# Three gate chunks per layer as seven block products in a streaming encoder on one Trainium2 core

## What is computed

```python
gates = jax.nn.sigmoid(g.reshape(bsz, t_len, N_BRANCH, D_MODEL) + b_gate)
merged = (gates[:, :, 0] * (y_a @ w_branch[0])
          + gates[:, :, 1] * (y_b @ w_branch[1])
          + gates[:, :, 2] * (y_c @ w_branch[2]))
x = layer_norm(DN_ALPHA * x + merged @ w_out, ln1_g, ln1_b)
```

## Time and profile before

| what | value |
|---|---|
| median of 3 runs | 1741.15 us (1741.02 to 1742.72) |
| the profiled execution's own time | 1741.31 us |
| its span | 1739.6 us |
| PE busy | 1725.9 us, 99% of the span, 13778 matmuls |
| DVE busy | 1365.6 us, 78% |
| ACT busy | 856.9 us, 49% |
| POOL busy | 101.6 us, 6% |
| DMA | 186.00 MB, mean 107 GB/s |

### The profile page before, as it was taken

How to read it: one execution, slowest core, us unless ns; L and a number is a source line. 1 busy time by engine, 2 the same in 40 slices (tenths; PEclk the granted TensorE clock), 3 DMA queues, 4 the chain that set the end, 5 groups by cost and what they waited for, 6 DMA issues and landing times.

```text
span 1739.6 us, 32719 instructions
## 1 busy us (share of the span) xinstructions
PE 1725.9 (99%) x13778; PEld 1692.2 (97%) x13778; DVE 1365.6 (78%) x1967; ACT 856.9 (49%) x1402; POOL 101.6 (6%) x159
## 2 busy tenths in 40 slices
PE   9999999999999999999999999999999999999997
PEld 9998899999999999999999989999999999999997
DVE  5698778664799999877667887777558999998675
ACT  4246532263366665645442565333535656656443
POOL 0025100000010000000000350000001000000000
PEclk9999999999999999999999999999999999999999
DMA  5432122222213222355524221223232222223554
GB/s 177 150 124 74 38 86 87 73 86 97 78 69 122 98 98 99 109 182 177 170 96 156 94 74 61 75 85 95 76 98 97 74 98 98 97 99 133 177 168 132
DMA packets 36514, 186.00 MB, mean 107 GB/s; under 512 B 7376, under 2 KB 11728, under 8 KB 18192
## 3 DMA queue, kind: packets, MB, share of 16 engines
q1 hardware_dynamic: 34672, 176.28, 30.2%
q10 hardware_dynamic: 1696, 7.64, 1.2%
HBM read 176.75 MB, written 7.15 MB: 106 GB/s over the span
## 4 chain that ended last, share of the span: by engine, by line
PE 93%; DVE 5%; DMA 1%; issue 1%; ACT 1%; ACTq 0%; DVEq 0%
PE acc L2086 22%; PE acc L2092 22%; PE acc L2091 22%; PE score L2086 5%; PE score L2092 5%; PE score L2091 5%; PE small L2091 1%; PE small L2092 1%; PE small L2086 1%; PE score L2173 1%; PE turned L2091 1%; PE turned L2092 1%; PE turned L2086 1%; PE small L2224 1%; PE turned L2204 1%; DVE acc L1421 1%
## 5 line engine op out<-in xcount | busy, mean ns | idle before, releaser
L2086 PE MATMUL acc<-xh,wh 128*128 128x272 f32 x1880 | 550.7, 293 | 1.3 <-DVE xl L1157 1.1
L2092 PE MATMUL acc<-xh,wl 128*128 128x272 f32 x1880 | 541.9, 288 | 0.0
L2091 PE MATMUL acc<-xl,wh 128*128 128x272 f32 x1880 | 540.9, 288 | 0.0
L2086 PEld LDWEIGHTS acc<-xh,wh 128*128 128x128 f32 x1880 | 354.0, 188 | 9.0 <-issue 5.0
L1203 DVE TENSOR_TENSOR wl<-raw,wh 128x2048 fp32r<-128x2048 f32 (+2 forms) x116 | 231.5, 1995 | 163.1 <-ACT wh L592 162.3
L2091 PEld LDWEIGHTS acc<-xl,wh 128*128 128x128 f32 x1880 | 354.1, 188 | 0.0
L2092 PEld LDWEIGHTS acc<-xh,wl 128*128 128x128 f32 x1880 | 353.2, 188 | 0.0
L592 ACT ACTIVATE wh<-raw 128x2048 fp32r<-128x2048 f32 (+2 forms) x136 | 232.8, 1712 | 159.9 <-DMA raw<-wdn 112.8
L2086 PE MATMUL acc<-fhh,wh 128*128 128x272 f32 x704 | 203.1, 288 | 0.3 <-DVE wl L1203 0.2
L2091 PE MATMUL acc<-fll,wh 128*128 128x272 f32 x704 | 202.5, 288 | 0.0
L2092 PE MATMUL acc<-fhh,wl 128*128 128x272 f32 x704 | 202.3, 287 | 0.0
(11 more groups left out here) (351 smaller groups left out, 3959.1 us busy)
## 6 DMA issues: line engine op xcount, KB each, us to landing
raw<-win SPq DMA_DIRECT2D x50, 1024.0 KB, 5.0
raw<-wup SPq DMA_DIRECT2D x44, 1024.0 KB, 5.0
raw<-wdn SPq DMA_DIRECT2D x32, 1024.0 KB, 4.9
raw<-wbr SPq DMA_DIRECT2D x24, 512.0 KB, 3.6
raw<-wdn SPq DMA_DIRECT2D x16, 768.0 KB, 4.2
raw<-wout SPq DMA_DIRECT2D x8, 1024.0 KB, 5.1
v_out<-vfm ACTq DMA_DIRECT2D x2, 1088.0 KB, 9.3
k_out<-k ACTq DMA_DIRECT2D x2, 1088.0 KB, 5.0
```

What stands on the lines that cost most here:

```text
L2086: first = mm(out, a, xs[0], start=start, stop=False, skip_group_check=onto)
L2091: mm(out, a, xs[1], start=False, stop=False, skip_group_check=onto)
L2092: return mm(out, b, xs[0], start=False, stop=stop, skip_group_check=onto)
```

## The change

- In the third branch, the gate chunks of pairs i = 1, 2 and 3 are done as seven block products, in the banks `score0` (GA), `small` (GB) and `score1` (GC). Pair 0 stays as it was. The units of w_branch stand between the products.
- The four differences of x are made by GpSimd in the second branch, behind the second variance (`ln_var`). Their high parts are ScalarE's and their low parts VectorE's, at the start of the third branch, with the weight sums of pair 1, all ahead of VectorE's products of pair 0.
- VectorE makes the sums, the low parts and three additions per chunk; ScalarE takes three snapshots and makes the four sigmoids, one of them (b = 2) from the bank, the others from sums in `tmp`.
- `conv_write` has one Silu pass, to `acc`; VectorE rounds it to `yah` with a copy, two tiles at a time, and subtracts.
- The squares of the convolution's norm move to another address; the differences lie where `acc`, `glu`, `gex` and `cbuf` were, so two zero columns of `gex` are written again per layer, and SP's last chunk of w_out waits for product 5 of pair 3.

The diff, cut to its core (indentation reduced; "..." marks what is left out):

```diff
-sqc = [sb("sqc0", [P, CT, HALF], at=F + 90016), sb("sqc1", [P, CT, HALF], at=F + 71168)]
+sqc = [sb("sqc0", [P, CT, HALF], at=F + 2 * T4), sb("sqc1", [P, CT, HALF], at=F + 2 * T4 + TB)]
+
+G = F + 69632
+G_LOW = {T1: G, T3: G + TB, T2: G + 5 * TB, T4N: GX}
+G_HIGH = {T1: G + 2 * TB, T3: G + 3 * TB, T2: G + 4 * TB, T4N: C}
+gth = {j: sb(f"gth{j}", [P, 4, HALF], F32R, at=G_HIGH[j]) for j in range(4)}
+gtl = {j: sb(f"gtl{j}", [P, 4, HALF], F32R, at=G_LOW[j]) for j in range(4)}
+gtraw = {j: sb(f"gtraw{j}", [P, 4, HALF], at=G_LOW[j]) for j in range(4)}
...
+GQ, GA, GB, GC = 3, bs[0], bo, bs[1]
+G_ORDER = {T4N: 1, T2: 2, T3: 3, T1: 4}
...
+                sp.wait_ge(gprod_full, 7 * gquad(l, 3) + 5)
...
+        pool.wait_ge(glu_stored, 16 * 2 * CT * (r + 1))
+        pool.wait_ge(ln_var, 2 * (r + 1))
+        x_at = [[xT[:, 4 * k_:4 * k_ + 4, dcol(h)] for h in range(2)] for k_ in range(2)]
+        for n, (j, a, b) in enumerate(((T1, x_at[0][1], x_at[0][0]), (T3, x_at[1][1], x_at[0][1]),
+                                       (T2, x_at[1][1], gtraw[T1][:, :, :]),
+                                       (T4N, x_at[1][0], gtraw[T2][:, :, :]))):
+            if n > 1:
+                pool.wait_ge(gt_made, 4 * r + (1 if n == 2 else 3))
+            g.tensor_tensor(gtraw[j][:, :, :], a, b, ALU.subtract).then_inc(gt_made, 1)
...
-                if n == 2 and b == 2:
...
+        def gate_first_blocks(i):
+            if i < 4:
+                s = SLOT[gate_chunk(l, i)]
+                assert turn[0] == gate_chunk(l, i)
+                turn[0] += 1
+                act.wait_ge(raw_full[s], c.take(raw_full[s], 16))
+                act.wait_ge(gs_made, 4 * gquad(l, i) + 2)
+                A(wh[s][:, 0:CHUNK // 2], raw[s][:, 0:CHUNK // 2], ACT.Copy).then_inc(hi_full[s], c.up(hi_full[s]))
...
+        def gate_turned_hi(j):
+            act.wait_ge(gt_made, 4 * (l + 1))
+            if j != T4N:
+                act.wait_ge(ya_full, 2 * CT * (l + 1))
+            A(gth[j][:, :, :], gtraw[j][:, :, :], ACT.Copy).then_inc(gt_hi, 1)
+
+        def make_ready(b):
+            if b == 1:
+                gate_turned_hi(T2)
+                gate_first_blocks(1)
+                gate_turned_hi(T3)
+            if b == 2:
+                gate_two_sums(1)
+                gate_second_blocks(1)
+            if b == 3:
+                gate_turned_hi(T1)
+                gate_last_sum(1)
...
+        def gate_snapshot(name, i, product):
+            act.wait_ge(gprod_full, 7 * gquad(l, i) + product)
+            A(snap[0][name][:, :], GA[:, 0:HALF], ACT.Copy).then_inc(gsnapped, 1)
...
+        def block_gates(i):
+            gate_snapshot("m1", i, 1)
+            hi()
+            gate_snapshot("u1", i, 3)
+            gate_sigmoid(i, 0, 1)
+            gate_snapshot("u3", i, 5)
+            gate_sigmoid(i, 3, 2)
+            if i == 3:
+                hi()
+            gate_first_blocks(i + 1)
+            gate_two_sums(i + 1)
+            gate_sigmoid(i, 2)
+            gate_last_sum(i + 1)
+            gate_second_blocks(i + 1)
+            gate_sigmoid(i, 1, 3)
...
                 A(acc[:, t, dcol(h)], sqc[h][:, t, :], ACT.Silu, scale=col(par, PAR["conv_g"] + t),
-                  bias=col(par, PAR["conv_bb"] + t))
-                A(ya[0][:, t, dcol(h)], sqc[h][:, t, :], ACT.Silu, scale=col(par, PAR["conv_g"] + t),
                   bias=col(par, PAR["conv_bb"] + t)).then_inc(ln_hi, c.up(ln_hi))
...
+                elif n == 2 and i:
+                    block_gates(i)
                 else:
-                    gates(i, n, mixed_hi if (n, i) == (0, 3) else squares if (n, i) == (1, 2) else None)
+                    gates(i, n, mixed_hi if (n, i) == (0, 3) else squares if (n, i) == (1, 2)
+                          else make_ready if n == 2 else None,
+                          first=(lambda: gate_turned_hi(T4N)) if n == 2 else None)
...
+            act.wait_ge(gex_zeroed, l + 1)
...
-    def conv_lo(h):
-        for t in range(CT):
-            dve.wait_ge(ln_hi, c.take(ln_hi))
+    def conv_parts(h):
+        two = [slice(2 * j, 2 * j + 2) for j in range(2)]
+        for t in two:
+            dve.wait_ge(ln_hi, c.take(ln_hi, 2))
+            v.tensor_copy(ya[0][:, t, dcol(h)], acc[:, t, dcol(h)]).then_inc(vec, c.up(vec))
+        for j, t in enumerate(two):
+            dve.wait_ge(vec, c.seen(vec, 1 - j))
             v.tensor_tensor(ya[1][:, t, dcol(h)], acc[:, t, dcol(h)], ya[0][:, t, dcol(h)].bitcast(F32),
-                            ALU.subtract).then_inc(ya_full, c.up(ya_full))
+                            ALU.subtract).then_inc(ya_full, c.up(ya_full, 2))
...
+        def gate_turned_lo(j):
+            dve.wait_ge(gt_hi, 4 * l + G_ORDER[j])
+            v.tensor_tensor(gtl[j][:, :, :], gtraw[j][:, :, :], gth[j][:, :, :].bitcast(F32),
+                            ALU.subtract).then_inc(gt_ready, 1)
...
+        def gate_three_sums(i):
+            if i < 4:
+                a11, a12, a21, a22 = gate_blocks(i)
+                j, q = gate_chunk(l, i), gquad(l, i)
+                dve.wait_ge(raw_full[SLOT[j]], 16 * (SLOT[:j + 1].count(SLOT[j]) - (1 if SLOT[j] < 2 else 0)))
+                if i > 1:
+                    dve.wait_ge(gprod_full, 7 * (q - 1) + 5)
+                v.tensor_tensor(gate_sum(0), a21, a22, ALU.add).then_inc(gs_made, 1)
+                dve.wait_ge(gs_made, 4 * q + 1)
+                v.tensor_tensor(a21, a11, a21, ALU.subtract).then_inc(gs_made, 1)
+                v.tensor_tensor(gate_sum(1), gate_sum(0), a11, ALU.subtract).then_inc(gs_made, 1)
...
+        def gate_add(i, b, bank, name, product, snapshot):
+            dve.wait_ge(gprod_full, 7 * gquad(l, i) + product)
+            dve.wait_ge(gsnapped, 3 * gquad(l, i) + snapshot)
+            dve.wait_ge(m_sum, c.seen(m_sum) if b != 1 else c.seen(m_sum, 1))
+            v.tensor_tensor(tmp[:, b, :], bank[:, 0:HALF], snap[0][name][:, :], ALU.add).then_inc(gcombined, 1)
+
...
+        def block_products(i):
+            def one(b):
+                t, cols = 2 * i + b % 2, (b // 2 * HALF, (b // 2 + 1) * HALF)
+                dve.wait_ge(gate_made, 4 * gquad(l, i) + (1, 4, 3, 2)[b])
+                dve.wait_ge(acc_full[b], c.take(acc_full[b]))
+                v.tensor_tensor(tmp[:, b, :], ps[b][:, 0:HALF], tmp[:, b, :], ALU.mult).then_inc(
+                    acc_free[b], c.up(acc_free[b]))
+                dve.wait_ge(acc_free[b], c.seen(acc_free[b]))
+                v.tensor_tensor(row(merged, t, *cols), row(merged, t, *cols), tmp[:, b, :], ALU.add).then_inc(
+                    m_sum, c.up(m_sum))
...
+            gate_add(i, 0, GB, "m1", 2, 1)
+            lo()
+            gate_add(i, 3, GC, "u3", 5, 3)
+            gate_three_sums(i + 1)
+            if i == 3:
+                lo()
+            one(0)
+            gate_fourth_sum(i + 1)
+            gate_first_low(i + 1)
+            gate_two_lows(i + 1)
+            gate_add(i, 1, GC, "u1", 7, 2)
+            one(1)
+            if i == 3:
+                low(0)
+                low(1)
+            gate_back_low(i + 1)
+            one(2)
+            one(3)
+            if i < 3:
+                low(0)
+                low(1)
+            gate_last_low(i + 1)
+            low(2)
+            low(3)
...
+        conv_parts(0)
         lo()
-        for h in range(2):
-            conv_lo(h)
-        lo()
+        conv_parts(1)
+        gate_three_sums(1)
+        gate_fourth_sum(1)
+        gate_turned_lo(T4N)
+        gate_turned_lo(T2)
+        gate_first_low(1)
+        gate_turned_lo(T3)
+        gate_two_lows(1)
+        gate_back_low(1)
+        gate_turned_lo(T1)
+        gate_last_low(1)
         products(0, 2)
-        for i in range(3):
-            lo()
-            lo()
-            products(i + 1, 2)
+        for i in range(1, 4):
+            block_products(i)
...
+        v.memset(gex[:, :, 0:2], 0.0).then_inc(gex_zeroed, 1)
...
-        for i in range(4):
-            chunk()
-            chunk(xs=ya, nk=CT, first=ya_tiles if i == 0 else None)
+        chunk()
+        chunk(xs=ya, nk=CT, first=ya_tiles)
+        pe.wait_ge(mixed_used, c.seen(mixed_used))
+
+        def gate_product(i, p, s):
+            q = gquad(r, i)
+            if p == 2:
+                pe.wait_ge(lo_full[s], c.take(lo_full[s]))
+            if i > 1 and p in (1, 2, 4):
+                pe.wait_ge(*{1: (gate_made, 4 * q - 1), 2: (gcombined, 3 * q - 2), 4: (gcombined, 3 * q)}[p])
+            if p in (3, 5, 6):
+                pe.wait_ge(gsnapped, 3 * q + {3: 1, 5: 2, 6: 3}[p])
+            if p in (3, 6):
+                pe.wait_ge(gs_ready, 2 * q + {3: 1, 6: 2}[p])
+            if p == 7:
+                pe.wait_ge(gcombined, 3 * q + 2)
+            turned = {3: T2, 4: T3, 5: T1, 7: T4N}.get(p)
+            if i == 1 and turned is not None:
+                pe.wait_ge(gt_ready, 4 * r + G_ORDER[turned])
+            bank = {2: GB, 4: GC, 7: GC}.get(p, GA)
...
```

(85 more changed lines are left out.)

50 lines of the change are left out of this document (49 added, 1 removed).

## The result

| what | before | after |
|---|---|---|
| median | 1741.00 us (17 runs, 1740.60 to 1742.82) | 1745.16 us (17 runs, 1742.54 to 1749.48) |
| ratio | | 1.0024, 95% interval 1.0017 to 1.0032 |
| profiled execution: time, span | 1741.31, 1739.6 us | 1745.37, 1743.6 us |

The changed kernel is slower by 4.2 us. It also scatters as the kernel before does not: 6.9 us between its fastest and its slowest run. That spread turns out to be more than half of the answer. The mean granted clock of each execution goes with its time: 0.998 for the three fastest (1742.54 to 1742.96 us), 0.997 for the next five (1743.97 to 1744.18), 0.996 for the three from 1745.16 to 1745.37, and 0.994 to 0.996 for the six above.

The account below looks back on a forecast made before the run. TensorE, busy 1725.9 of 1739.6 us, was taken as the bound. Per layer -4.52 + 1.75 + 0.26 + 0.68 + 1.3 = -0.5 us, twice -1.1 against 1741.31, gave 1740.2 us, range 1736.5 to 1746.5.

Parts of the forecast that it names:

- slower by over 0.2%: Outcome given chance 0.25: 0.2 from slow GpSimd subtractions plus 0.05 from TensorE's clock falling.
- GpSimd's D: Time of one GpSimd subtraction of 1088 columns, taken as 2.2 us; slower rival from 2.77 on, 1747.5 at 3.1, chance 0.2.
- What is removed: Third branch's gate chunks: 12 matmuls less per chunk, 72 in all at 0.1255 us, 9.04 us, 4.52 a layer.
- Start of block work: Pair 1, product 3: TensorE waits 1.75 us a layer for snapshot m1, listed behind ScalarE's fourth rounding.
- the ledger: The prediction's walk through the engines' lists, pricing waits by the instructions in front; sum -0.5 us a layer.
- the slide of 1.1: VectorE's list at the start of block work shifts 1.1 us later because GpSimd's subtractions delay its earlier work.
- GpSimd: Second branch: VectorE waits for GpSimd's four subtractions, 1.3 us a layer; chunk 30's low part 0.2 us late.
- Pairs 2 and 3: Product 3 of each pair wanted at 12.05 us, snapshot m1 done at 12.18: 0.13 us lost each.
- Output chunks: Low part of chunk 39 late because chunk 38's stands ahead of pair 3's products: 0.68 us a layer.
- what I called no change: A time within 0.2% (3.5 us) of the kernel before, the limit of what a measurement can tell.
- The clock: Rival: standing still 2.9 us before product 3 lowers TensorE's clock to 1.2 GHz; 3 us a layer, 1746, chance 0.05.

Follow-up runs that it names:

- the filler kernel: The changed kernel plus 20 matmuls of 272 columns into an idle bank before product 3 of pair 1, results unread; 1742.38 us, ratio 1.0010.

## Why the prediction was wrong

I had forecast 1740.2 us, 1736.5 to 1746.5, and gave "slower by over 0.2%" one chance in four. 1745.16 lies in the range, but on the side that I had held less likely, and by the rival to which I gave 0.05: the other 0.2 of that one chance in four stood on GpSimd's D at 2.77 us or more, which the trace does not show. That the range, drawn for D near 3, holds the result is luck. Point by point:

- **What is removed** (4.52 us a layer): right. 13706 matmuls, pitch 0.1255.
- **Start of block work**: the order, snapshot m1 behind pair 0's roundings, was named and is where the largest wait stands. I expected 1.75 + 1.1 = 2.85 us of lateness; it was 2.96 - 0.1255 = 2.84. VectorE's products of pair 0 began at 392.44, for 391.3 by the ledger (390.2 and the slide of 1.1); TensorE was itself 1.06 us late by then, 0.33 of it from the start of the kernel, and the two cancel. The rounding of 544 columns took 0.79 / 2 = 0.4 us, as I had read it.
- **GpSimd**: the mechanism was right (VectorE waits for a whole GpSimd instruction), the size was not. D was 2.4, not 2.2: taken in proportion from 512 columns it came out short. Chunk 30 was late by 0.86 - 0.1255 = 0.74 us, not 0.2. **This is the first term that was mis-sized**: 0.54 us a layer. The estimate from the Trainium skill that stood beside it (GPSIMD Engine Reference, section "Elementwise — side-by-side cycle accounting"), 2.39 us, agrees with the trace's 2.4.
- **Pairs 2 and 3**: 0.15 each for 0.13. **Output chunks**: 0.69 for 0.68.
- **The restart.** Behind each of these waits the second matmul comes 0.23 us after the first: 0.10 us at five places a layer, which I did not count. The trace of before has it (behind its wait of 0.36 us at 299.0 us the second matmul follows after 0.23); my rows did not. **The second term**: 0.5 us a layer.

These two make 2 x 1.04 = 2.1 us, and with them the ledger gives 1742.3. That is what the changed kernel does when the clock stays up: its fastest runs, 1742.54 to 1742.96, and the filler kernel's 1742.38. It is slower than before by 0.08%, inside what I called no change.

- **The clock** was the step that failed: in the sum it stood at nothing, and it makes 2.8 us of the median (1745.16 against the filler kernel's 1742.38). I gave it a chance of 0.05, on the ground that the granted clock was 1.00 through a stretch of 2 us without matmul, and that no row showed it restored behind a longer one. Both were true, and the second should have counted as much as the first: 2.9 us lay outside what the trace had shown. My price, 24 matmuls and 3 us a layer, was near (26 and 2.6). What I had not thought of is that it is a matter of chance. By their times and mean granted clocks only 3 of the 17 runs had no fall, and five more (1743.97 to 1744.18, 0.997) no more than a short one of 1.5 us, here or in the attention. The median, 1745.16, is what one long fall in one layer makes: 1742.6 + 2.6, as in the profiled execution.

So the gain was turned into new waits, 5.09 us a layer where I had forecast 3.99 of the 4.52 saved, and what carried the median past 0.2% is the clock's answer to the longest of them.

## What to carry to other kernels

On a kernel that TensorE bounds, removing matmuls pays only as far as the hand-written lists of the other engines keep up; walk each list and ask which short instruction that TensorE waits for stands behind long ones that can wait. Moving one snapshot of 0.4 us per pair gave back 7.4 us, some 5.2 of waits and the rest most likely of clock. Price a standstill of TensorE above what its trace shows as harmless twice, once for its length and once for the clock, and keep GpSimd's instructions short wherever VectorE works beside them.
